# Attention score products of a head pair, alternating between the lower and the upper 64 rows of the array

## The chip, the cores and the metric

The kernel runs on one core of a Trainium2 chip. The metric is the device time of one execution in microseconds. Before the change the median of three runs is 2363.9 us (2360.26 to 2368.31). The five engines of the core work from queues of their own and meet through semaphores: TensorE (PE; its weight loads are listed apart as PEld), VectorE (DVE), ScalarE (ACT), GpSimd (POOL) and SyncE (SP), which here only starts DMAs.

## The reference, cut to what matters

One layer, 512 prompt tokens and 32 sample tokens, width 1024. The part that the change touches is the attention over the prompt: three groups of eight heads of 64 channels, each group with a window and a dilation of its own, and one softmax over the keys of all three groups of a head slot.

```python
HEAD_DIM = 64
HEADS_PER_GROUP = 8
GROUP_WINDOWS = (128, 512, 2048)
GROUP_DILATIONS = (1, 4, 16)
...
    s = jnp.einsum('brnqhe,brnkhe->brnhqk', qb, kb, preferred_element_type=F32) * (HEAD_DIM ** -0.5)
    s = jnp.where(mask[None, None, :, None], s, -jnp.inf)
    lse = jax.nn.logsumexp(s, axis=-1)
    p = jnp.exp(s - lse[..., None]).astype(v.dtype)
    o = jnp.einsum('brnqhk,brnkhe->brnqhe', p, vb).reshape(b, dilation, mp, h, e)[:, :, :m]
...
def finish_layer(x, heads_out, conv_out, gates, w_attn_proj, w_out, norm2_w,
                 w_peer_q, peer_sub_keys, expert_u, expert_v):
    attn_out = heads_out.reshape(b, t, ATTN_OUT_WIDTH) @ w_attn_proj
    mixed = gates[:, :, 0] * conv_out + gates[:, :, 1] * attn_out
    x1 = x + mixed @ w_out
    h2 = rms_norm(x1, norm2_w)
    return x1 + peer(h2.reshape(b * t, D_MODEL), w_peer_q, peer_sub_keys,
                     expert_u, expert_v).reshape(b, t, D_MODEL)
```

The last step, `peer`, gathers 128 experts per token from a table of 16384 rows. All arithmetic is float32.

## The kernel before

The 512 prompt tokens are four tiles of 128 (t = 0 to 3); the 32 sample tokens are a fifth, `NT`. Work runs in two phases: phase 0 takes tiles 0, 1 and `NT` through the whole layer up to the expert search, phase 1 takes tiles 2 and 3. The gathers of the experts (544 steps of 128 rows of 8 KB) of tiles 0, 1 and `NT` run beside phase 1, those of tiles 2 and 3 mostly after it.

`plan()` (L204) writes out the order of all work by hand as a list of ticks. A tick holds one `mm` entry (usually two of the eight slices of a projection) and whatever other tasks were put on it. Each engine walks through all the ticks in order and does its own part of each task; inside a tick the tasks stand by the rank in `RANK` (L199): the projection first, the score task `S` after `T` (turn the weights), `O` (weights times values), `H` and `M`. `pe_cost` and `step_marks` (L395, L403) spread the gather steps over the ticks: `MARK[n]` is the number of gather steps that PE has to have done by tick n.

Attention goes by head slot x = 8t + 2hp + w: hp is one of four pairs, w one of two heads of a pair. The queries and keys of a pair lie in the same tiles, head 0 on partitions 0 to 63 and head 1 on 64 to 127, so a score product contracts over 64 rows. `rounds(t)` (L101) cuts the key blocks of a slot into rounds of at most four blocks (512 columns, one PSUM bank): two rounds for tiles 0 to 2, three for tile 3. For each round `scores` (L1151) on PE waits until its bank is free, multiplies the runs of neighbouring blocks into it and raises `s_ready`; DVE scales, masks and copies the bank to `s_sb` (L1931). There are two score banks, `sbk`, used in turn by every user of the pool (`SB`, made by `bank_uses`, L496): `S`, and also `DS` (sample attention), `L1`, `L2`, `W` and `SC`. After the last round DVE takes the maximum (`M`, L1941), ACT the exponential (L1586), PE turns the weights (L1343) and multiplies the values (L1173).

In `plan()` the loop over w (L279) puts the rounds of head 0 on consecutive ticks from `at`, its `M` on the next, and then the rounds of head 1. For the first pair of tile 0 this is: rounds of head 0 at ticks 65 and 66, `M` at 67, rounds of head 1 at 68 and 69, `M` at 70; tile 1 follows with 71, 72, 73 and 74, 75, 76. The four pairs of phase 0 start 27 ticks apart, those of phase 1 24 ticks apart (from tick 322 on). `first` (L297), the tick from which the sample attention of phase 0 (`DS`, `DN`, `DM`, `DT`, `DV`, `DE`, `DH`) and the norm of the sample tokens are put, is the tick after the last `M`: 158.

```python
                    for w in range(2):
                        x = HG * t + 2 * hp + w
                        for r in range(len(rounds(t))):
                            put(at + r, ("S", x, r))
                        at += len(rounds(t))
                        put(at, ("M", x))
```

The q and k projections go through two banks `zb`. The reader that frees such a bank is `q2` on DVE (L1907), put three ticks after the end of the projection; POOL computes its scale in `q1` (L1038, L1039) from a sum that DVE makes (L1896).

Of the kernel before, what the change touches and what calls it, by code (L numbers as in the profile page):

```python
# [13 lines left out]
P = 128  # L14
# [8 lines left out]
HD, HG, NG = 64, 8, 3  # L23
# [77 lines left out]
def rounds(t):  # L101


    g1 = [(1, u) for u in range(t + 1)]
    g2 = [(2, t)] + [(2, u) for u in range(t)]
    g0 = [(0, u) for u in (t - 1, t) if u >= 0]
    if t == 3:
        return [(0, g1), (6, g2), (4, g0)]
    return [(3 - t, g1 + g0[:-1]), (5, g0[-1:] + g2)]
# [18 lines left out]
def turn_groups(t):  # L128
    return -(-len(blocks_of(t)) // 4)
# [6 lines left out]
def pair(x):  # L136

    t, r = divmod(x, HG)
    return t, r // 2, r % 2
# [64 lines left out]
def plan():  # L204
# [5 lines left out]
    def put(tick, task):  # L210
        tasks.setdefault(int(tick), []).append(task)
# [26 lines left out]
    for p in range(2):  # L238
# [21 lines left out]
        free_at = 0  # L260
        for hp in range(HP):
            for ty in range(3):
                for t, e in each(p, "qkv", hp, ty):
                    if ty < 2:
                        put(e + 1, ("q1", t, hp, ty))
                        put(e + 3, ("q2", t, hp, ty))
                        put(e + 4, ("q3", t, hp, ty))
                        put(e + 6, ("Q", t, hp, ty))
                        if ty == 1:
                            put(e + 6, ("ko", t, hp))  # L270
                        continue
                    put(e + 1, ("v", t, hp))
                    put(e + 2, ("vo", t, hp))
                    if p == 0 and t != NT:
                        put(e + 4, ("hs", t, hp))
                    if t == NT:
                        continue
                    at = max(e + 4, free_at)
                    for w in range(2):  # L279
                        x = HG * t + 2 * hp + w  # L280
                        for r in range(len(rounds(t))):
                            put(at + r, ("S", x, r))
                        at += len(rounds(t))
                        put(at, ("M", x))
                        for q in range(turn_groups(t)):
                            put(at + 2 + q, ("T", x, q))
                        put(at + 3 + turn_groups(t), ("O", x))
                        put(at + 4 + turn_groups(t), ("E", x))
                        last = at + 6 + turn_groups(t)
                        at += 1  # L290
                    free_at = at
                    put(last, ("H", x))
            if p and hp < 2:
                put(last + 1, ("hl", hp + 2))
            if p == 0 and hp == 2:
                put(now, ("kv", 0))
        first = free_at  # L297
        for q in range(4):
            for t, e in each(p, "gate", q):
                put(e + 1, ("g", t, q))  # L300
# [224 lines left out]
ZB, SB, TB, OB = bank_uses()  # L525
# [68 lines left out]
def program(nc, a, sc):  # L594
    with ExitStack() as ctx:
# [45 lines left out]
        qT = qTs[:, :].rearrange("p (a b g t) -> p a b g t", a=2, b=2, g=NG)  # L641
        kT = kvr[:, 0:8 * QW].rearrange("p (a g t) -> p a g t", a=2, g=NG)
# [72 lines left out]
        sbk = [ps("s0"), ps("s1")]  # L715
# [10 lines left out]
        s_ready, s_free = sem("s_ready"), [sem("s_free_v"), sem("s_free_a")]  # L726
# [40 lines left out]
        def bank_free(eng, pool, by_sems, key):  # L767
            at = pool.before(key)
            if at is not None:
                eng.wait_ge(by_sems[at[0]], at[1])  # L770
# [333 lines left out]
        def _(eng):  # L1104
# [44 lines left out]
                    mm.then_inc(z_ready, 1)  # L1149

            def scores(x, r):  # L1151
                t, hp, w = pair(x)
                lo = HD * w
                if r == 0:
                    eng.wait_ge(tp_free, TB.no["Q", t, hp, 1] + 1)
                    if t % 2:
                        eng.wait_ge(tp_free, TB.no["Q", t - 1, hp, 1] + 1)
                    if t >= 2 and w == 0:
                        eng.wait_ge(hist_in[hp % 2], 32 * (hp // 2 + 1))
                bank_free(eng, SB, s_free, ("S", x, r))  # L1160
                bank = sbk[SB.bank(("S", x, r))]
                for at, g, u, c in runs(rounds(t)[r][1]):
                    mm = eng.matmul(bank[:, P * at:P * (at + c)], qT[lo:lo + HD, hp % 2, t % 2, g, :], kT[lo:lo + HD, hp % 2, g, P * u:P * (u + c)], start=True, stop=True)  # L1163
                mm.then_inc(s_ready, 1)

            def weigh(x):
                t, hp, w = pair(x)
# [130 lines left out]
            for n, tick in enumerate(TICKS):  # L1298
                for v in tick:
                    if v[0] == "mm":  # L1300
                        multiply(*v[1:])
                    elif v[0] == "XT":
                        t, q = v[1:]
# [4 lines left out]
                        for j in range(4):  # L1308
                            mm = eng.transpose(tpb[:, P * j:P * j + m], rows[:, 512 * q + P * j:512 * q + P * (j + 1)], cst[0:m, C_ID:C_ID + m])
                        mm.then_inc(tp_ready, 1)  # L1310
                    elif v[0] == "U":
                        t, c = v[1:]
# [3 lines left out]
                        if t == NT:  # L1316
                            for r in range(QUAD):
                                lo = 64 * (r % 2)
                                mm = eng.matmul(tpb[lo:lo + 64, P * (r // 2):P * (r // 2) + SMP], ub[:, i % 2, 0:64], ident[:, SMP * r:SMP * (r + 1)], start=True, stop=True)
# [13 lines left out]
                                mm = eng.transpose(tpb[:, P * g:P * (g + 1)], qkr[:, t % 2, ty, P * g:P * (g + 1)], ident)  # L1333
                        mm.then_inc(tp_ready, 1)
                    elif v[0] == "S":
                        scores(*v[1:])
                    elif v[0] == "T":
                        x, q = v[1:]
                        nb = len(blocks_of(pair(x)[0]))
# [768 lines left out]
```

## Time and profile before

| what | value |
| --- | --- |
| median of 3 runs | 2363.9 us |
| the profiled execution's own time | 2364.97 us |
| its span, first to last instruction | 2363.1 us |
| PE busy | 1678.2 us (71%) |
| DVE busy | 1468.1 us (62%) |
| mean granted TensorE clock | 0.801 |

The profiled execution lies 1.1 us above the median and 1.9 us above its own span. A view by stretches tells at what share of its time each engine was busy and which clock PE had; the list of waits tells who waited for whom; the timeline gives starts and durations in order; the chain follows the work that ended last back to what released it. The end of a matmul is modelled and includes its drain, so what a group of matmuls costs in the stream is read from its start to the start of the next group.

### The profile page before, as it was taken

To read this page: it belongs to the slowest core of one execution; us is meant where nothing else is said; L and a number is where in the kernel's file an instruction comes from. 1 tells how busy PE (TensorE), PEld (TensorE's weight loads), DVE (VectorE), ACT (ScalarE), POOL (GpSimd) and SP (SyncE) were. 2 spreads that over 40 slices of the span, in tenths; PEclk is the share of its full clock that TensorE was granted. 3 is DMA by queue.
4 is the path that set the end of the run, shared out by engine and by line. 5 is a ranking of instruction groups with operands and counts; after the bars stand their busy time and mean duration, and the time that the engine had idled before them with its cause. 6 is when DMAs were issued, how large, how long until landed. Compare 5 with 4: busy or idle time off the path is not lost.

```text
span 2363.1 us, 32781 instructions
## 1 busy us (share of the span) xinstructions
PE 1678.2 (71%) x11544; PEld 770.1 (33%) x11544; DVE 1468.1 (62%) x3591; ACT 882.9 (37%) x2386; POOL 750.7 (32%) x713
## 2 busy tenths in 40 slices
PE   6988899998788887777788889885433343343343
PEld 3455565444334443433444433331000000000000
DVE  1466656212556777777878676535676765676764
ACT  2122123201444544544455662333343333343332
POOL 1244100000222334433343333323444443344342
PEclk9998999999889998898889999996555555555555
DMA  4333435645889888899989999999999999999998
GB/s 170 137 105 105 158 111 216 263 182 191 310 345 383 345 350 326 314 347 358 339 343 359 367 394 397 404 407 371 408 391 405 401 392 376 400 387 399 403 386 362
DMA packets 130191, 756.64 MB, mean 320 GB/s; under 512 B 16836, under 2 KB 42940, under 8 KB 50268
## 3 DMA queue, kind: packets, MB, share of 16 engines
q0 software_dynamic: 78336, 570.46, 61.5%
q1 hardware_dynamic: 51692, 184.09, 21.0%
q8 instruction: 92, 1.51, 0.2%
q14 instruction: 71, 0.58, 0.1%
HBM read 734.70 MB, written 20.64 MB: 320 GB/s over the span
## 4 chain that ended last, share of the span: by engine, by line
DMA 20%; DVE 15%; PE 9%; issue 6%; ACT 3%; POOL 0%; DVEq 0%; POOLq 0%; ACTq 0%
DMA ring<-in_expert_uv,pick 20%; PE z L1141 4%; DVE ring L1843 4%; PE acc L1292 3%; DVE cand L1785 1%; DVE e L1786 1%; DVE cand L1783 1%; DVE ti L1748 1%; DVE ti L1751 1%; DVE sco L1749 1%; ACT wgt L1455 1%; ACT fold L1457 1%; DVE tv L1750 1%; DVE ci L1751 1%; DVE ci L1748 1%
## 5 line engine op out<-in xcount | busy, mean ns | idle before, releaser
L1073 POOL DMA_INDIRECT ring<-in_expert_uv,pick x544 | 628.1, 1155 | 1012.2 <-PE acc L1292 935.1
L1843 DVE CUSTOM_DVE_ANT_0 ring<-ring,rep 128x1024 f32<-128x1024 f32 x544 | 660.3, 1225 | 379.1 <-DMA ring<-in_expert_uv,pick 354.5
L1292 PE MATMUL acc<-ring,fold 128*32 128x256 f32 x4352 | 464.0, 517 | 496.9 <-ACT fold L1457 495.0
L1141 PE MATMUL z<-wts,hT 128*128 128x384 f32 (+1 forms) x1408 | 628.4, 583 | 31.7 <-DVE tmp L1907 25.3
L1453 ACT ACTIVATE gel<-dots 128x1 f32<-128x1 f32 x544 | 109.8, 202 | 790.7 <-DVE dots L1843 783.2
L1292 PEld LDWEIGHTS acc<-ring,fold 128*32 128x32 f32 x4352 | 105.3, 126 | 822.1 <-ACT fold L1457 746.8
L1141 PEld LDWEIGHTS z<-wts,hT 128*128 128x128 f32 x1408 | 263.8, 203 | 288.6 <-issue 229.4
L1141 PE MATMUL z<-wts,yT 128*128 128x512 f32 x384 | 192.2, 636 | 14.3 <-ACT yT L1631 7.0
L1457 ACT ACTIVATE fold<-cst,wgt 128x32 f32<-128x32 f32 x544 | 174.8, 321 | 17.7
L1455 ACT ACTIVATE wgt<-gel,pick 128x1 f32<-128x1 f32 x544 | 160.3, 295 | 17.7
L1740 DVE SCALAR_TENSOR_TENSOR yT<-uT,vec,yT 128x256 f32<-128x256 f32 x240 | 109.2, 504 | 2.0
L1141 PEld LDWEIGHTS z<-wts,yT 128*128 128x128 f32 x384 | 70.8, 199 | 102.0 <-issue 101.9
L1931 DVE SCALAR_TENSOR_TENSOR sx<-s,cst 128x512 f32<-128x512 f32 (+3 forms) x72 | 40.2, 558 | 97.8 <-PE s L1163 91.0
L1038 POOL TENSOR_SCALAR xss<-xss 128x1 f32<-128x1 f32 (+1 forms) x10 | 1.9, 194 | 302.1 <-ACT kvr L1646 247.9
L1453 ACT ACT_TABLE_LOAD x69 | 88.5, 1283 | 1.2
L1038 POOL TENSOR_SCALAR ssq<-ssq 128x6 f32<-128x6 f32 (+1 forms) x40 | 15.4, 386 | 196.7 <-DVE ssq L1896 196.1
L1163 PE MATMUL s<-kvr,qTs 64*128 64x128 f32 (+3 forms) x272 | 68.0, 369 | 0.0
L1466 ACT ACTIVATE pt<-t 128x512 f32<-128x512 f32 (+2 forms) x64 | 33.4, 522 | 79.0 <-PE t L1343 79.0
L1173 PEld LDWEIGHTS o<-kvr,pt 128*128 128x128 f32 x432 | 55.2, 200 | 17.9 <-issue 11.0
L1173 PE MATMUL o<-kvr,pt 128*128 128x64 f32 x432 | 54.4, 279 | 8.1 <-DVEq L1810 5.8
L1343 PE MATMUL t<-cst,sx 128*128 128x128 f32 x216 | 39.5, 303 | 21.3 <-ACT hoT L1466 17.1
L1039 POOL TENSOR_TENSOR ssq<-ssq,half_m 128x6 f32<-128x6 f32 (+1 forms) x40 | 49.8, 1246 | 3.5 <-POOL ssq L1038 0.2
(219 smaller groups left out, 1745.2 us busy)
## 6 DMA issues: line engine op xcount, KB each, us to landing
wts<-in_w_qkv SPq DMA_DIRECT2D x24, 1536.0 KB, 8.2
wts<-in_w_glu SPq DMA_DIRECT2D x8, 2048.0 KB, 12.2
wts<-in_w_gate SPq DMA_DIRECT2D x8, 2048.0 KB, 11.6
wts<-in_w_wq SPq DMA_DIRECT2D x8, 2048.0 KB, 11.7
ring<-in_k_cache SPq DMA_DIRECT2D x8, 1536.0 KB, 9.4
ring<-in_v_cache SPq DMA_DIRECT2D x8, 1536.0 KB, 8.1
rep<-x_h SPq DMA_DIRECT2D x68, 128.0 KB, 9.9
ring<-in_expert_uv,pick POOLq DMA_INDIRECT x544, 11.3
```

The source lines that it names most:

```text
L1039: return eng.tensor_tensor(to, to, half_m[0:m, 0:w], ALU.pow)
L1073: eng.indirect_dma_start(ring[:, i % RING, :], None, a["expert_uv"], bass.IndirectOffsetOnAxis(picks(i, 0).bitcast(U32), 0)).then_inc(row_ ...
L1141: mm = eng.matmul(bank[:, 0:w], of[:, k, :], rows[:, k, :], start=(k == 0), stop=(k == depth - 1))
L1163: mm = eng.matmul(bank[:, P * at:P * (at + c)], qT[lo:lo + HD, hp % 2, t % 2, g, :], kT[lo:lo + HD, hp % 2, g, P * u:P * (u + c)], start=T ...
L1173: mm = eng.matmul(ob[:, 0:HD], pt[:, P * j:P * (j + 1)], vv[:, hp % 2, u, P * g + HD * w:P * g + HD * (w + 1)], start=(j == 0), stop=(j == ...
L1292: mm = eng.matmul(acc[b][SUB * c:SUB * (c + 1), col:col + 256], fold[:, i % 4, :], ring[:, i % RING, D + 256 * c:D + 256 * (c + 1)], start ...
L1453: eng.activation(gel[:, i % 4:i % 4 + 1], dots[:, i % 4:i % 4 + 1], ACT.Gelu).then_inc(gel_ready, 1)
L1455: eng.activation(wgt[:, i % 4:i % 4 + 1], gel[:, i % 4:i % 4 + 1], ACT.Copy, scale=picks(i, 1)).then_inc(wgt_ready, 1)
L1457: eng.activation(fold[:, i % 4, :], cst[:, C_FOLD:C_FOLD + SUB], ACT.Copy, scale=wgt[:, i % 4:i % 4 + 1]).then_inc(fold_ready, 1)
L1740: ins = eng.scalar_tensor_tensor(out=out, in0=src, scalar=cw[:, c, tap:tap + 1], in1=out, op0=ALU.mult, op1=ALU.add)
L1748: link(eng.max_index(index[:, 0:8], values[:, 0:8], x))
L1843: eng.tensor_tensor_reduce(u, u, rep[:, j, :], 1.0, 0.0, ALU.mult, ALU.add, dots[:, i % 4:i % 4 + 1]).then_inc(dot_ready, 1)
```

## The change

In the planner the rounds of both heads of a pair are put on the same ticks, first head then second, and the `M` and later tasks of the second head follow the first head's by one tick and as many ticks as the first head has turns (`turn_groups`: 1 for tile 0, 2 for tiles 1 and 2, 3 for tile 3). `free_at` keeps the next tile behind the turns of the second head. `first` becomes the tick after the last score round. On PE the `S` entry of the second head does nothing; the entry of the first head waits for both banks and issues the products of both heads in turn, run by run: head 0 from rows 0 to 63 into its bank, head 1 from rows 64 to 127 into the other. One increment by 2 on the last product tells DVE of both. DVE's copies are unchanged but for their ticks.

```diff
--- before.py
+++ after.py
@@ -276,25 +276,28 @@
                     if t == NT:
                         continue
                     at = max(e + 4, free_at)
+                    for r in range(len(rounds(t))):
+                        for w in range(2):
+                            put(at + r, ("S", HG * t + 2 * hp + w, r))
+                            scored = at + r + 1
                     for w in range(2):
                         x = HG * t + 2 * hp + w
-                        for r in range(len(rounds(t))):
-                            put(at + r, ("S", x, r))
-                        at += len(rounds(t))
+                        if w == 0:
+                            at += len(rounds(t))
                         put(at, ("M", x))
                         for q in range(turn_groups(t)):
                             put(at + 2 + q, ("T", x, q))
                         put(at + 3 + turn_groups(t), ("O", x))
                         put(at + 4 + turn_groups(t), ("E", x))
                         last = at + 6 + turn_groups(t)
-                        at += 1
-                    free_at = at
+                        at += 1 + (1 - w) * turn_groups(t)
+                    free_at = at + turn_groups(t)
                     put(last, ("H", x))
             if p and hp < 2:
                 put(last + 1, ("hl", hp + 2))
             if p == 0 and hp == 2:
                 put(now, ("kv", 0))
-        first = free_at
+        first = scored
         for q in range(4):
             for t, e in each(p, "gate", q):
                 put(e + 1, ("g", t, q))
@@ -1149,19 +1152,22 @@
                     mm.then_inc(z_ready, 1)
 
             def scores(x, r):
-                t, hp, w = pair(x)
-                lo = HD * w
+                t, hp, _ = pair(x)
                 if r == 0:
                     eng.wait_ge(tp_free, TB.no["Q", t, hp, 1] + 1)
                     if t % 2:
                         eng.wait_ge(tp_free, TB.no["Q", t - 1, hp, 1] + 1)
-                    if t >= 2 and w == 0:
+                    if t >= 2:
                         eng.wait_ge(hist_in[hp % 2], 32 * (hp // 2 + 1))
-                bank_free(eng, SB, s_free, ("S", x, r))
-                bank = sbk[SB.bank(("S", x, r))]
+                banks = []
+                for w in range(2):
+                    bank_free(eng, SB, s_free, ("S", x + w, r))
+                    banks.append(sbk[SB.bank(("S", x + w, r))])
                 for at, g, u, c in runs(rounds(t)[r][1]):
-                    mm = eng.matmul(bank[:, P * at:P * (at + c)], qT[lo:lo + HD, hp % 2, t % 2, g, :], kT[lo:lo + HD, hp % 2, g, P * u:P * (u + c)], start=True, stop=True)
-                mm.then_inc(s_ready, 1)
+                    for w in range(2):
+                        lo = HD * w
+                        mm = eng.matmul(banks[w][:, P * at:P * (at + c)], qT[lo:lo + HD, hp % 2, t % 2, g, :], kT[lo:lo + HD, hp % 2, g, P * u:P * (u + c)], start=True, stop=True)
+                mm.then_inc(s_ready, 2)
 
             def weigh(x):
                 t, hp, w = pair(x)
@@ -1333,7 +1339,8 @@
                                 mm = eng.transpose(tpb[:, P * g:P * (g + 1)], qkr[:, t % 2, ty, P * g:P * (g + 1)], ident)
                         mm.then_inc(tp_ready, 1)
                     elif v[0] == "S":
-                        scores(*v[1:])
+                        if pair(v[1])[2] == 0:
+                            scores(*v[1:])
                     elif v[0] == "T":
                         x, q = v[1:]
                         nb = len(blocks_of(pair(x)[0]))
```

## Rows read from the trace of the kernel before

**Rows 1.** The stretches: us, busy time (instructions) by engine, PEclk, DMA share, GB/s.

```profile
138.00:355.00 217.00, 198.57 (x1243) 129.60 (x1242) 130.37 (x309) 50.80 (x117) 50.85 (x71) 0.93 0.36 122
355.00:575.00 220.00, 211.59 (x1485) 106.20 (x1487) 65.07 (x138) 44.28 (x80) 2.23 (x6) 1.00 0.58 216
...
880.00:1320.00 440.00, 346.77 (x1960) 176.17 (x1956) 342.06 (x863) 221.87 (x534) 169.45 (x142) 0.87 0.90 340
...
1625.00:2363.00 738.00, 294.74 (x2296) 62.43 (x2296) 488.37 (x1184) 264.94 (x868) 303.64 (x264) 0.52 0.99 390
```

**Rows 2.** Waits of PE, then of DVE, from 138 to 355 us: total, times, longest.

```profile
PE z L1141 <- DVE tmp L1907: 16.5, 6, 3.5
...
DVE sx L1931 <- PE s L1163: 52.9, 29, 6.0
```

**Rows 3.** Waits of PE, then of DVE, from 880 to 1320 us.

```profile
PE acc L1292 <- ACT fold L1457: 28.4, 14, 4.4
...
DVE sx L1931 <- PE s L1163: 38.1, 20, 7.0
```

**Rows 4.** The score products (L1163) alone in two stretches: PE busy, PEld busy.

```profile
138.00:355.00 217.00, 24.34 (x128) 17.76 (x128) 0.93 0.36 122
880.00:1320.00 440.00, 43.61 (x144) 21.34 (x144) 0.87 0.90 340
```

**Rows 5.** Timeline of PE, phase 0: start, us, line, tile, shape, count.

```profile
155.54 0.93 PE L1163 MATMUL s<-kvr,qTs 64*128 64x128 f32 x6
156.41 0.91 PE L1141 MATMUL z<-wts,hT 128*128 128x384 f32 x2
```

**Rows 6.** Timeline of PE, phase 1: a score product and four products on 32 columns.

```profile
1201.02 0.70 PE L1163 MATMUL s<-kvr,qTs 64*128 64x256 f32 x2
1201.65 0.64 PE L1292 MATMUL acc<-ring,fold 128*32 128x256 f32 x8
1202.22 0.59 PE L1141 MATMUL z<-wts,hT 128*128 128x384 f32 x1
```

**Rows 7.** Timeline, DVE and PE, around PE's wait in phase 0.

```profile
161.93 0.56 DVE L1931 SCALAR_TENSOR_TENSOR sx<-s,cst 128x384 f32<-128x384 f32 x1
...
164.08 0.56 DVE L1931 SCALAR_TENSOR_TENSOR sx<-s,cst 128x384 f32<-128x384 f32 x1 [0.22 <-PE s L1163]
...
166.84 0.55 DVE L1907 TENSOR_TENSOR tmp<-z,ssq 128x384 f32<-128x384 f32 x1
...
167.53 0.98 PE L1141 MATMUL z<-wts,hT 128*128 128x384 f32 x1 [3.49 <-DVE tmp L1907]
```

**Rows 8.** Chain that ended last, second heads' score products, from 1116 us: start, us.

```profile
1151.92 1.06 PE s L1163 x4
1155.48 1.09 PE s L1163 x6
...
1197.11 1.08 PE s L1163 x4
...
1309.86 1.06 PE s L1163 x4
1314.28 0.64 PE s L1163 x2
```

**Rows 9.** Timeline, PE and DVE: two rounds of a head and the copy between.

```profile
1161.46 1.12 PE L1163 MATMUL s<-kvr,qTs 64*128 64x512 f32 x2
...
1169.34 1.13 PE L1163 MATMUL s<-kvr,qTs 64*128 64x128 f32 x4
...
1169.71 0.69 DVE L1931 SCALAR_TENSOR_TENSOR sx<-s,cst 128x512 f32<-128x512 f32 x1
```

**Rows 10.** Who waited for DVE's copies (L1931) in the whole run.

```profile
  PEld s L1163: 0.2, 1
```

**Rows 11.** Waits of PE from 355 to 575 us.

```profile
PE s L1190 <- DMA ring<-in_k_cache: 2.0, 1, 2.0
```

**Rows 12.** DMA issues of the page: loads, KB each, median us from issue to landing.

```profile
wts<-in_w_gate SPq DMA_DIRECT2D x8, 2048.0 KB, 11.6
```

## Prediction

> **What bounds the kernel now.** I read the stretches first: they say where PE sets the pace. From 138 to 355 us lie the projections of phase 0 with its attention. PE is busy for 198.6 of 217 us there, DVE for 130 and the DMA engines for 0.36 of the time; from 355 to 575 us PE is busy for 211.6 of 220 us [rows 1]. So phase 0 goes at PE's pace, and what PE saves there moves everything behind it, unless a wait of PE takes it. The list of waits has one that matters: PE waits 16.5 us in six places for DVE to free a projection bank [rows 2]. From 880 to 1320 us, the attention of phase 1, no engine is full: PE 347 of 440 us, DVE 342, DMA share 0.90 [rows 1]. PE waits there for weights that come of the gathers (28.4 us), and DVE in turn waits 38.1 us in 20 places for score products [rows 3]. From 1625 us on the DMA share is 0.99 [rows 1]: a fixed number of gathers, which the change doesn't touch. A gain can only come out of the two attention stretches, and it shifts the tail as a whole.
>
> **The score products.** By the view of L1163 alone they take 24.3 us of PE in phase 0 and 43.6 us in phase 1 [rows 4]. These times hold drains: a round of 0.93 us is followed by the next group after 0.87 [rows 5], one of 0.70 after 0.63 [rows 6], so 0.07 us of each round isn't stream time. There are 32 rounds in phase 0 (four pairs, two tiles, two heads, two rounds) and 40 in phase 1 (tile 3 has three): 24.3 - 2.2 = 22.1 us and 43.6 - 2.8 = 40.8 us.
>
> The change leaves as many products, but sends them in pairs to separate halves of the array's rows. No row of this trace has two products on different rows at once, so the cost is bounded from both sides. Nothing gained: the two halves run one after the other, and the saving is 0. Everything gained: a pair of rounds costs what one does, and half is saved, 11.0 and 20.4 us. A cost above today's is the fourth case below. The nearest row is one on columns: eight instructions of 256 columns on four strips of 32 columns start and give way to the next group within 0.57 us (1201.65 to 1202.22), while two instructions of 256 columns on 64 rows and all columns took 0.63 us (1201.02 to 1201.65) [rows 6]. So four float32 products in four parts of the array cost what one does, and they are issued in turn, part by part, as the change does it with rows. I take the upper end, half. The Trainium skill (TensorE: Matmul & The Clock Gate, Part 3: Packing small matmuls — row/col tiling) gives 3.07 times for four row tiles, less than the full four; as an estimate from that page two tiles would give 1.54 times, a saving of 35% instead of half, and the forecast's gain of 17 us would be about 12. No run so far shows row tiles.
>
> **Phase 0: what of 11.0 us reaches the end.** PE sets the pace, so all of it, except where PE waits afterwards for something that hasn't become earlier. That is the wait of 3.49 us at 167.53 us [rows 7], right behind the score rounds of tile 1's second head; it occurs in three of the four pairs (the fourth has gates behind it, whose bank DVE doesn't free). PE waits for DVE's q2 (166.84 us). Before that DVE does two score copies of 0.56 us, one at 161.93 and one at 164.08 us, the second after waiting for PE [rows 7]. In the new order both copies come three ticks earlier, where DVE is ahead of PE anyway (it waits for PE in 29 of the 32 rounds of phase 0, 52.9 us [rows 2]), so q2 comes 1.1 us earlier. PE comes to the wait about 1.7 us earlier (two rounds of 0.87 [rows 5]). The wait keeps 0.6 us of each, 1.8 us in three. Left: 11.0 - 1.8 = 9.2 us.
>
> **Phase 1: what of 20.4 us reaches the end.** The chain that ended last can be followed back to 1116 us, so it covers pairs 2 and 3. Of the second heads' ten rounds there, which are what pairing folds away, five stand on the chain: 1.06 + 1.09 + 1.08 + 1.06 + 0.64 = 4.9 us [rows 8]. The others stand beside DVE's or ACT's work, which is late next, and bring nothing. For all four pairs I take twice that, 9.9 us; the ends are 0 (the gathers and DVE set the pace, DMA share 0.90) and 20.4.
>
> **The new wait.** Today a round waits for the copy made two rounds earlier; DVE's copies have held up PE for 0.2 us in the whole run [rows 10]. In the new order a pair takes both banks, and the next round, one tick later, needs both copies done. Behind the waiting product PE holds the next projection slices, the gather products and the turns; for those wait ACT, DVE and, for its ring buffers, POOL. Phase 0: two copies of 0.56 us [rows 7] are 1.1 us; the tick between holds four projection instructions, of which two take 0.91 us with their drain [rows 5], so they cover it and the cost is 0. Without that cover it would be 1.1 us in each of eight places, 9 us, the whole gain of phase 0. Phase 1 has twelve such places. The longest lag of DVE: the round that starts at 1161.46 and streams for 1.06 us is copied only from 1169.71 on, 7.2 us later; with two copies of 0.69 us the banks would be free after 8.6 us, and PE comes to the next round after 6.8 us (1169.34) [rows 9]. That is 1.8 us here; elsewhere the lag is shorter and the tick covers it. I take 2 us; bounds 0 and the fourth case.
>
> **Small parts.** The sample attention and the norm of the sample tokens of phase 0 start at tick 154 instead of 158 with their distances kept; the cache loads that SP starts behind them, and SP's waits for them, move along. One of these loads now comes ahead of the weights of the last gate unit (ticks 165 and 166), which PE needs nine ticks later; a gate load lands 11.6 us after its issue [rows 12], and nine ticks of four instructions at some 0.4 us [rows 5] are over 14 us without the sample products between them. PE's one wait there for a key cache is 2.0 us [rows 11], so -2 to +2, taken as 0. In phase 1 tile 3's attention lies two ticks later; its turns, values and the history load for pair hp+2 that SP starts after it have more than ten ticks to spare before their users. Gather steps shift by a few ticks with the score cost; their number and their sum stay. The increment by 2 lets DVE start on the first head only when both are done; with the halves side by side that is nothing. Where PE gains time but then waits, its granted clock, 0.87 in this stretch [rows 1], may fall; 0.01 of it is at most 347 x 0.01 / 0.87 = 4 us of PE's busy time there, in either direction; taken as 0.
>
> **The sum.** 9.2 + 9.9 - 2 = 17.1 us. From the profiled execution's own 2364.97 us: 2347.9. That execution lies 1.1 us above the median of 2363.9, so against the median the forecast is -16 us, 0.7%. About 0.3% (7 us) is what a measurement of this kernel can tell from no change.
>
> **The rivals.** First: the halves overlap, but phase 1 gives nothing. For it speak the DMA share of 0.90, PE's 28.4 us of waiting for weights from the gathers and the fact that DVE is as busy as PE [rows 1, 3]; against it that five second-head rounds stand on the chain [rows 8]. 2365 - 9 = 2356 us.
>
> Second: the change doesn't do what it says, row halves don't overlap. PE's stream stays at 22.1 and 40.8 us. For it: no row shows it. Against: the column strips [rows 6]. 2365 us, give or take 4 for the moved copies and the two banks.
>
> Third: phase 1 passes on all: 2365 - 9 - 20 + 2 = 2338 us.
>
> Fourth, slower: two banks used at once take the place of the double buffer, and PE waits for DVE. If DVE were as far behind in all twelve places of phase 1 as at 1161.46 us, the banks would be free after 8.6 us. PE comes back after 6.8 us in the eight places of tile 3 [rows 9] and in the four of tile 2 after a tick of four projection instructions and one gather group, 4 x 0.45 + 0.57, about 2.3 us [rows 5, 6]: 8 x 1.8 + 4 x 6.3 = 40 us, less 17: 2388 us. It decides from 1.4 us per place on (17 / 12). Against it: DVE waited for PE, not PE for DVE, in 20 of these 40 rounds [rows 3]. The Trainium skill (TensorEngine Tiling (Array Packing), PSUM Bottleneck) warns of just that: a faster array leaves the copy out of PSUM as the bottleneck. By that rule it would be this case; by DVE's 52.9 us of waiting for PE in phase 0 [rows 2] the copies there have room.
>
> **Chances.** Forecast 0.55, phase 1 nothing 0.17, no overlap 0.15, all passed on 0.05, slower 0.08. A time more than 7 us below the median means under 2357: nearly all of the forecast, half or more of the first rival and the third: 0.53 + 0.11 + 0.05 = 0.69. Within 7 us: 0.02 + 0.06 + 0.11 = 0.19. Slower: 0.04 + 0.08 = 0.12. The range from 2335 to 2366 takes in the forecast, the first and third rivals and half of the second.
>
> **What the profile would show.** Right: pairs of score instructions of the two halves start within a few hundredths of a microsecond, L1163's busy time falls from 68 us to about 36, the sample attention starts 8 to 10 us earlier, and the stretch from 575 to 1625 us shrinks by about as much again. The new wait would stand as PE or PEld s L1163 <- DVE sx, under 5 us. Wrong: L1163's time stays (second rival), the tail starts no more than 9 us earlier (first), or PE's waits for DVE's copies reach 17 us (fourth).

## The result and the profile after

The changed kernel takes 2342.09 us in the median of five runs (2335.23 to 2347.16) against 2363.9 before (now five runs too, 2360.26 to 2374.4). The ratio of the two is 0.9894, with a 95% interval from 0.9868 to 0.992: faster by about 1%, 22 us in the medians and 25 by the ratio. The forecast was 16 us, to 2348. The profiled execution took 2339.12 us, with a span of 2337.3 us and a mean granted clock of 0.797.

The lines move by a few: the scores are L1169, their copies L1938, the projections L1144, the expert products L1298, `q2` L1914, the dot products of the gathered rows L1850. First the stretches of the changed kernel, cut where the work of [rows 1] is done (columns as there):

```profile
138.00:350.00 212.00, 191.37 (x1284) 122.33 (x1283) 134.10 (x322) 49.65 (x114) 51.60 (x70) 0.93 0.37 127
350.00:565.00 215.00, 207.59 (x1438) 104.68 (x1440) 60.11 (x126) 45.47 (x81) 2.22 (x6) 1.00 0.58 218
...
865.00:1300.00 435.00, 340.26 (x2039) 171.42 (x2037) 352.59 (x894) 231.11 (x557) 165.49 (x149) 0.88 0.93 359
...
1600.00:2337.00 737.00, 292.08 (x2288) 61.56 (x2288) 486.61 (x1182) 264.70 (x867) 304.76 (x264) 0.52 0.99 390
```

The tail is as long as before and as full (DMA share 0.99, as in [rows 1]); it only starts earlier. Phase 0 is still PE's. In the attention of phase 1 the DMA share has risen from 0.90 to 0.93.

The score products alone in the two attention stretches, PE and PEld busy, against 24.34 and 43.61 us in [rows 4]:

```profile
138.00:350.00 212.00, 12.28 (x128) 9.04 (x128) 0.93 0.37 127
865.00:1300.00 435.00, 22.25 (x144) 10.68 (x144) 0.88 0.93 359
```

Half, in both. PE's timeline shows it on single rounds, one of phase 0 and one of phase 1:

```profile
153.45 0.94 PE L1169 MATMUL s<-kvr,qTs 64*128 64x128 f32 x12
154.32 1.56 PE L1144 MATMUL z<-wts,hT 128*128 128x384 f32 x4
...
943.16 0.70 PE L1169 MATMUL s<-kvr,qTs 64*128 64x256 f32 x4
943.79 0.64 PE L1298 MATMUL acc<-ring,fold 128*32 128x256 f32 x8
```

Twelve instructions of both heads (two for each product) take 0.87 us from their start to the next group's, as six of one head did in [rows 5]; four take 0.63 us, as two did in [rows 6]. In the records of the single instructions the partner on the other rows starts in most pairs 6 to 8 ns after its neighbour.

PE's wait for a projection bank, which [rows 7] show at 3.49 us, on the timeline of the changed kernel (DVE's `q2`, then PE):

```profile
163.16 0.56 DVE L1914 TENSOR_TENSOR tmp<-z,ssq 128x384 f32<-128x384 f32 x1
...
163.86 1.91 PE L1144 MATMUL z<-wts,hT 128*128 128x384 f32 x4 [3.56 <-DVE tmp L1914]
```

and its total in the list of PE's waits from 138 to 350 us (total, times, longest):

```profile
PE z L1144 <- DVE tmp L1914: 17.6, 6, 4.0
```

The three waits of that kind are now 3.56, 3.96 and 3.81 us; before, each was 3.49. The total has grown from 16.5 to 17.6 us [rows 2].

What `q2` itself waits for has changed. The end of POOL's scale and DVE's maximum of the second head in the kernel before, where `q2` starts at 166.84 us [rows 7]:

```profile
163.78 1.33 POOL L1039 TENSOR_TENSOR ssq<-ssq,half_m 128x6 f32<-128x6 f32 x1
...
165.26 0.95 DVE L1941 TENSOR_REDUCE nm<-sx 128x1 f32<-128x768 f32 x1
```

and in the changed one, where it starts at 163.16:

```profile
161.50 1.44 POOL L1042 TENSOR_TENSOR ssq<-ssq,half_m 128x6 f32<-128x6 f32 x1
...
161.98 0.95 DVE L1948 TENSOR_REDUCE nm<-sx 128x1 f32<-128x768 f32 x1
```

Before, `q2` came 1.7 us after the scale was done (165.11; spans on POOL are rough), behind the maximum; now it comes 0.2 us after it (162.94), and the maximum runs beside POOL's work.

Who waited for DVE's score copies, in the whole run (total, times), against 0.2 us once in [rows 10]:

```profile
  PEld s L1169: 4.8, 7
  PE s L1169: 1.1, 1
```

The first line is that of PE's weight loads (PEld), the second that of its products, and the two are not to be added up. The weight load and the product of the round at 1125.79 us wait for the same copies:

```profile
1125.76 0.78 PEld L1169 LDWEIGHTS s<-kvr,qTs 64*128 64x128 f32 x12 [1.14 <-DVE sx L1938]
1125.79 1.15 PE L1169 MATMUL s<-kvr,qTs 64*128 64x128 f32 x12 [1.08 <-DVE sx L1938]
```

The other six weight loads are like the first one in phase 0, whose products (153.45 us, above) waited for nothing:

```profile
153.45 0.75 PEld L1169 LDWEIGHTS s<-kvr,qTs 64*128 64x128 f32 x12 [0.55 <-DVE sx L1938]
```

In all six the products start 0.42 or 0.52 us after the last projection instruction, as score rounds behind such instructions did before. So DVE's copies hold up PE's products for 1.1 us in one place of phase 1, and nowhere else.

How long DVE waits for score products, first in phase 0 (138 to 350 us), then in phase 1 (865 to 1300 us); before, it was 52.9 and 38.1 us [rows 2, 3]:

```profile
DVE sx L1938 <- PE s L1169: 39.9, 16, 7.7
...
DVE sx L1938 <- PE s L1169: 11.4, 5, 5.1
```

Where the time was gained is best read from the dot products of the gathered rows, since their first one needs the expert search of phase 0 done and their last one stands at the end of the tail. This is their line in the kernel before (shortest, median and longest in ns, then first and last start in us):

```profile
L1843 DVE CUSTOM_DVE_ANT_0 ring<-ring,rep x544: 1211/1225/1296, 595.2 to 2355.6; 128x1024 f32<-128x1024 f32 x182
```

and in the changed one:

```profile
L1850 DVE CUSTOM_DVE_ANT_0 ring<-ring,rep x544: 1210/1225/1297, 585.6 to 2329.8; 128x1024 f32<-128x1024 f32 x182
```

Phase 0 gave 9.6 us (595.2 to 585.6). From the first dot to the last the run is another 16.2 us shorter; since the medians differ by 22 us and the two profiled executions by 26, phase 1 gave some 12 to 16 us.

### The profile page after: what moved, and what is told of

It reads as the page before. It is cut to its first block, busy times and chain, and to the rows that moved or that the text cites. A ratio compares the mean times of both kernels' runs of the same rounds, so it can differ in the third digit from the quotient of the medians.

```text
span 2337.3 us, 32787 instructions
## 1 busy us (share of the span) xinstructions
PE 1648.7 (71%) x11544; PEld 752.6 (32%) x11544; DVE 1465.3 (63%) x3591; ACT 883.0 (38%) x2386; POOL 745.9 (32%) x713
## 4 chain that ended last, share of the span: by engine, by line
PE 35%; DMA 27%; DVE 24%; issue 8%; ACT 4%; POOL 2%; SPq 0%; DVEq 0%; POOLq 0%; ACTq 0%
DMA ring<-in_expert_uv,pick 24%; PE z L1144 21%; DVE ring L1850 6%; PE acc L1298 4%; DMA sx<-in_x_prompt 2%; PE z L1150 2%; PE o L1179 1%; PE o L1232 1%; DVE cand L1792 1%; DVE e L1793 1%; DVE ti L1755 1%; PE s L1196 1%; DVE ti L1758 1%; DVE sco L1756 1%; DVE cand L1790 1%
## 5 line engine op out<-in xcount | busy, mean ns | idle before, releaser
L1076 POOL DMA_INDIRECT ring<-in_expert_uv,pick x544 | 614.9, 1130 | 998.6 <-PE acc L1298 920.5
L1850 DVE CUSTOM_DVE_ANT_0 ring<-ring,rep 128x1024 f32<-128x1024 f32 x544 | 660.3, 1225 | 387.9 <-DMA ring<-in_expert_uv,pick 357.4
L1298 PE MATMUL acc<-ring,fold 128*32 128x256 f32 x4352 | 460.6, 514 | 503.5 <-ACT fold L1464 501.8
L1144 PE MATMUL z<-wts,hT 128*128 128x384 f32 (+1 forms) x1408 | 627.6, 584 | 38.1 <-DVE tmp L1914 31.9
L1298 PEld LDWEIGHTS acc<-ring,fold 128*32 128x32 f32 x4352 | 105.0, 125 | 825.7 <-ACT fold L1464 756.2
L1144 PEld LDWEIGHTS z<-wts,hT 128*128 128x128 f32 x1408 | 265.8, 203 | 296.4 <-issue 238.4
L1144 PE MATMUL z<-wts,yT 128*128 128x512 f32 x384 | 191.2, 633 | 13.2 <-ACT yT L1473 6.4
L1144 PEld LDWEIGHTS z<-wts,yT 128*128 128x128 f32 x384 | 70.2, 198 | 100.0 <-issue 99.9
L1041 POOL TENSOR_SCALAR ssq<-ssq 128x6 f32<-128x6 f32 (+1 forms) x40 | 20.5, 513 | 193.3 <-DVE ssq L1903 192.7
L1938 DVE SCALAR_TENSOR_TENSOR sx<-s,cst 128x512 f32<-128x512 f32 (+3 forms) x72 | 36.8, 552 | 53.3 <-PE s L1169 51.3
L1042 POOL TENSOR_TENSOR ssq<-ssq,half_m 128x6 f32<-128x6 f32 (+1 forms) x40 | 52.9, 1322 | 3.5 <-POOL ssq L1041 0.2
L1593 ACT ACTIVATE sx<-sx,nm 128x384 f32<-128x384 f32 (+3 forms) x32 | 32.5, 1015 | 52.6 <-DVE nm L1949 52.5
## 6 DMA issues: line engine op xcount, KB each, us to landing
ring<-in_expert_uv,pick POOLq DMA_INDIRECT x544, 11.3
```

The source lines that it names most:

```text
L1042: return eng.tensor_tensor(to, to, half_m[0:m, 0:w], ALU.pow)
L1076: eng.indirect_dma_start(ring[:, i % RING, :], None, a["expert_uv"], bass.IndirectOffsetOnAxis(picks(i, 0).bitcast(U32), 0)).then_inc(row_ ...
L1144: mm = eng.matmul(bank[:, 0:w], of[:, k, :], rows[:, k, :], start=(k == 0), stop=(k == depth - 1))
L1298: mm = eng.matmul(acc[b][SUB * c:SUB * (c + 1), col:col + 256], fold[:, i % 4, :], ring[:, i % RING, D + 256 * c:D + 256 * (c + 1)], start ...
L1850: eng.tensor_tensor_reduce(u, u, rep[:, j, :], 1.0, 0.0, ALU.mult, ALU.add, dots[:, i % 4:i % 4 + 1]).then_inc(dot_ready, 1)
```

## Experiments

Every kernel was compared with runs of the kernel before on its own chip, where the median of before was 2371.5, 2367.7 or 2366.3 us; so the ratios are what can be set side by side. "Changed" is the kernel with the change.

**Both heads on the same rows.** The planner's new order, the pairs and the two banks stay; only the overlap is taken away, in both phases.

```diff
-                        lo = HD * w
+                        lo = 0
```

> The changed kernel, but the products of both heads are taken from rows 0 to 63 (so the second head's scores are those of the first); order, banks, waits and ticks are those of the changed kernel. Theory (the gain is the overlap of the row halves): the score products cost PE some 63 us of stream again, twice the changed kernel's, and the time is that of the kernel before, 2364 us, within 5. Rival (the gain comes of the new order of the ticks: DVE's copies earlier, fewer places where DVE waits for PE): most of the 22 us stay, 2342 to 2350 us.

Measured: 2352.58 us, ratio 0.9924 [0.9898, 0.995], 18 us by the ratio, of the 25 or 26 of the change. The stream of the scores in the two stretches:

```profile
138.00:352.00 214.00, 20.15 (x128) 16.62 (x128) 0.93 0.34 117
865.00:1330.00 465.00, 40.69 (x144) 23.12 (x144) 0.88 0.92 356
```

and the round on PE's timeline that answers to the twelve instructions above:

```profile
153.79 1.60 PE L1169 MATMUL s<-kvr,qTs 64*128 64x128 f32 x12
155.33 1.24 PE L1144 MATMUL z<-wts,hT 128*128 128x384 f32 x3
```

On the same rows the twelve instructions take 1.54 us instead of 0.87, so the overlap is real, and it is the rows that bring it. But the order alone is already faster than before, and has more than half of the gain. Two things were seen at once. In phase 0, of the 12.1 us of busy time that the scores lost (24.34 to 12.28), 4.2 came of pairing without any overlap (24.34 to 20.15). About 1.1 of these are the drains of 16 groups fewer, 0.07 us each as the prediction counts them, and 3 are stream: two rounds apart cost twice 0.87 us, a pair on the same rows 1.54, so what lies between groups is paid once instead of twice. And the other part of this kernel's gain has little to do with the stream: the scores of phase 1 are still busy for 40.69 us here (36.8 and 36.5 in the two runs below with the same phase 1; three rounds took 4.2 us longer here).

**The same rows in phase 1 only.** The overlap of phase 0 stays. It ran twice, on two chips.

```diff
-                        lo = HD * w
+                        lo = HD * w if t < 2 else 0
```

> The changed kernel with both heads' products from rows 0 to 63 in phase 1 alone (tiles 2 and 3), so that the halves overlap in phase 0 only; the second head's scores of tiles 2 and 3 are the first's. Theory (9 to 10 us of the gain are phase 0's, the rest is stream time saved in phase 1): 2354 us. Rival (phase 1's gain is not the stream time but the new order): 2342 to 2346 us.

> The kernel with both heads of tiles 2 and 3 taken from rows 0 to 63 once more, now beside the changed kernel on one chip. Theory A (the first runs' reading: phase 1's gain comes of the new order, in which DVE waits for PE in fewer places and a pair pays the first weight load and the switch behind it once, not of the overlap): within 4 us of the changed kernel. Theory B (the forecast's: half of the stream saved reaches the end): the stream in phase 1 is 12 us longer than in the changed kernel, so 6 us slower than that; if all of it reaches the end, 12 us.

> The changed kernel itself, measured beside the next three on one chip. All theories: about 1% below the kernel before on the same chip.

Measured: 2346.03 us, 0.9888 [0.9859, 0.9918], and beside the changed kernel itself 2342.51 us, 0.99 [0.9883, 0.9916], where the changed kernel had 2340.04 us, 0.9889 [0.9867, 0.991]. The score products of phase 1 in the second run of this kernel:

```profile
865.00:1330.00 465.00, 36.48 (x144) 21.11 (x144) 0.89 0.93 357
```

and in the changed kernel beside it:

```profile
865.00:1330.00 465.00, 21.58 (x144) 10.69 (x144) 0.87 0.93 357
```

PE streams 14.9 us more, and the end comes 2.5 us later in the medians; the single executions of the two kernels put the difference between -3 and 7 us, so it isn't told from 0, and half of the stream, 7.4 us, lies at the edge. The first run of this kernel, at 0.9888, isn't slower than the change either. So in phase 1 the overlap itself brings little, and nothing that can be measured here. Against the kernel with the same rows in both phases, on its chip, the first run is 6.6 us faster (2352.58 to 2346.03) for the 7.9 us of stream that differ in phase 0. The dot products of these two kernels, same rows in both phases first:

```profile
L1850 DVE CUSTOM_DVE_ANT_0 ring<-ring,rep x544: 1212/1225/1294, 590.7 to 2343.3; 128x1024 f32<-128x1024 f32 x182
...
L1850 DVE CUSTOM_DVE_ANT_0 ring<-ring,rep x544: 1211/1225/1294, 584.3 to 2339.3; 128x1024 f32<-128x1024 f32 x182
```

Their first one comes 6.4 us earlier with the overlap in phase 0: there most of the saving does reach the end. With the old phase 0 it starts on the same chip at 595.7 us (the next experiment), so without any overlap the new order already gives 5 us of phase 0.

**The change in one phase only.** A function of the tile decides between the changed order with its pairs and the old one, here for phase 0, with the opposite condition for phase 1.

```diff
+def paired(t):
+    return t < 2
...
+                    if paired(t):
+                        for r in range(len(rounds(t))):
+                            for w in range(2):
+                                put(at + r, ("S", HG * t + 2 * hp + w, r))
...
+                    else:
+                        for w in range(2):
+                            x = HG * t + 2 * hp + w
+                            for r in range(len(rounds(t))):
+                                put(at + r, ("S", x, r))
```

> Pairs in phase 0 alone; tiles 2 and 3 keep the plan and the products of the kernel before. Theory: 9 to 10 us less than before, 2354 us, and the tail of gathers starts some 10 us earlier than before. Rival (the halves' gain of phase 0 is swallowed by the gathers behind it): 2360 us or more.

> Pairs in phase 1 alone; tiles 0 and 1 keep the plan and the products of the kernel before. By the forecast's own step (half of 20 us reaches the end, less 2 us of waits) 2356 us. By the profile after (phase 1 gave 16 us) 2348 us. If the profiled run was an outlier of the kernel, in between: 2352 us.

Measured: phase 0 only, 2362.68 us, 0.9964 [0.9944, 0.9984], 8.5 us by the ratio; phase 1 only, 2353.68 us, 0.9934 [0.9909, 0.9958], 15.6 us. Together they make the whole (0.9964 x 0.9934 = 0.9898; the change measured 0.9894 and 0.9889). The dot products with phase 0 only, the first 9.7 us earlier than before, the last only 1.4:

```profile
L1888 DVE CUSTOM_DVE_ANT_0 ring<-ring,rep x544: 1211/1225/1298, 585.5 to 2354.2; 128x1024 f32<-128x1024 f32 x182
```

and with phase 1 only, the first where it was, the last 8.9 us earlier:

```profile
L1888 DVE CUSTOM_DVE_ANT_0 ring<-ring,rep x544: 1210/1225/1297, 595.7 to 2346.7; 128x1024 f32<-128x1024 f32 x182
```

The first starts fit phase 0: with the old one they are 593.1 to 595.7 us in three profiled executions, with the changed one 579.8 to 585.6 in seven, of which the two under 584 had a granted clock of 0.95 and 0.96 from 130 to 356 us, all the others 0.93. The last ones stand for one execution each, and scatter as the executions do (2351.9 to 2370.5 us for the first of the two kernels), so the sizes are taken from the ratios.

**The old order, tile 3's attention two ticks later.** The kernel before, with nothing paired and no overlap; only the distance that the change puts ahead of tile 3 is kept.

```diff
-                    at = max(e + 4, free_at)
+                    at = max(e + 4, free_at + 2 * (t == 3))
```

> The kernel before with tile 3's attention put two ticks later, as the change does by the way, and nothing else of the change. Theory (DVE's fewer waits are what phase 1 gains by): no difference from the kernel before, within 4 us. Rival (the spacing is what gains): 8 us or more below it.

Measured: 2359.32 us, 0.9963 [0.9946, 0.9979], 8.8 us by the ratio. An edit of one line to the kernel before, which removes no work, is worth as much as all of phase 0. DVE's waits for scores don't explain it: in phase 1 they are 43.7 us in 18 places here and 38.1 in 20 before [rows 3]. What differs is another wait, at the products that spread an index list into the output bank that DVE's normalised heads (`ho`) free. On the timeline of the kernel before, the longest of them:

```profile
1017.80 0.28 DVE L1951 TENSOR_SCALAR ho<-o,rden 128x64 f32<-128x64 f32 x1
...
1018.14 0.29 PE L1274 MATMUL o<-cand,cst 32*32 32x8 f32 x8 [7.36 <-DVE ho L1951]
```

its line in that kernel's list of PE's waits from 865 to 1330 us:

```profile
PE o L1274 <- DVE ho L1951: 13.5, 3, 7.4
```

and the same line with tile 3 two ticks later:

```profile
PE o L1274 <- DVE ho L1951: 1.3, 2, 0.8
```

It goes through all the kernels: the one with the change in phase 0 only, whose phase 1 is the old one, has 13.3 us of it in three places; in the changed kernel and those with the same rows, the change in phase 1 only or other small shifts it is 2.6 us at most. So the spacing moves the spread out of the way of a head that isn't normalised yet. That this one wait is the whole 8.8 us is not shown: PE's wait for the experts' weights fell too (28.4 to 15.1 us), and no run took the one away without the other. Nor does any run take the two ticks out of the changed kernel; that they are worth as much there is assumed.

**Another two ticks, in the changed kernel.** The same edit once more, on top of the change.

> The changed kernel with tile 3's attention another two ticks later. If spacing as such pays (the old order gained 0.37% by it), another 4 to 8 us below the changed kernel. If only the first two ticks pay, because they take tile 3's first copies away from tile 2's turns, no difference (within 3 us).

Measured: 2344.51 us, 0.9895 [0.9872, 0.9918]: no further gain, as follows if the wait at the spread was already gone. It showed something else. Who waited for DVE's copies:

```profile
  PEld s L1169: 11.3, 8
  PE s L1169: 7.1, 3
```

PE's products wait 7.1 us in three places, against 1.1 in one; eight weight loads show 11.3 us, three of them in the same three places. That is less than the 17 us at which the prediction would have given up its forecast, but six times the wait of the changed kernel, and the time is that of the changed kernel. So either such waits cost nothing that can be measured, or the added ticks gained what the waits cost; no run separates the two. DVE waits 23.7 us for scores here, twice as long as in the changed kernel.

**Pairs of rounds two ticks apart in phase 1.** A tick of projection and gather work more between two pairs, so that DVE has done both copies.

```diff
-                            put(at + r, ("S", HG * t + 2 * hp + w, r))
-                            scored = at + r + 1
+                            put(at + gap(t) * r, ("S", HG * t + 2 * hp + w, r))
+                            scored = at + gap(t) * r + 1
...
-                            at += len(rounds(t))
+                            at += gap(t) * (len(rounds(t)) - 1) + 1
```

with `gap(t)` 1 for tiles 0 and 1 and 2 for the others.

> The changed kernel with the rounds of a pair two ticks apart instead of one in phase 1, so that DVE has two ticks to free both banks. The profile after shows PE's products waiting for DVE's copies 5.9 us in 8 places; these should go. Forecast's fourth case in small: at most 4 us below the changed kernel, more likely within 3 of it, as the maxima come later by one or two ticks.

Measured: 2353.46 us, 0.9944 [0.992, 0.9968], over half a percent slower than the changed kernel (0.9889). Who waited for the copies:

```profile
  PEld s L1174: 2.4, 4
```

and in the list of waits of phase 1, DVE's for scores and PE's for the experts' weights:

```profile
DVE sx L1943 <- PE s L1174: 26.6, 8, 6.8
...
PE acc L1303 <- ACT fold L1469: 45.0, 24, 6.4
```

No product waits for the copies any more (1.1 us in the changed kernel; the 2.4 us are the four weight loads of phase 0, whose products don't wait), and the stream is as short as in the changed kernel (21.03 us), yet time is lost. The edit also ends the scores and puts the maxima one tick later for tile 2 and three for tile 3, whose attention starts a tick later besides (the expectation has one or two ticks, and takes the new wait at 5.9 us), and more waiting stands at the experts' weights (45.0 us, 31.5 in the changed kernel over the same stretch); that the one leads to the other is likely and not shown. At any rate the change's new wait is cheaper than this way to avoid it.

**Head by head.** The two loops inside a round are exchanged: all products of the first head, then all of the second, on their own rows and banks, without alternation.

```diff
-                for at, g, u, c in runs(rounds(t)[r][1]):
-                    for w in range(2):
+                for w in range(2):
+                    for at, g, u, c in runs(rounds(t)[r][1]):
```

> The changed kernel with the loops over runs and heads exchanged: all products of the first head of a round, then all of the second, on their own rows; nothing else differs. If PE overlaps only neighbours in its order, rounds with one run keep the overlap, those with two or three overlap at one place only: L1163's stream would be about 14 of 22 us in phase 0 and 28 of 41 in phase 1 instead of 11 and 23, and the time 3 to 5 us above the changed kernel. If PE looks further ahead, no difference.

Measured: 2343.16 us, 0.9901 [0.9884, 0.9918]; the changed kernel beside it had 0.9889. The stream in both stretches:

```profile
130.00:352.00 222.00, 13.63 (x128) 10.45 (x128) 0.94 0.38 130
865.00:1330.00 465.00, 22.88 (x144) 11.85 (x144) 0.88 0.93 359
```

and on PE's timeline a round of two runs a head, then one of three:

```profile
148.81 0.93 PE L1169 MATMUL s<-kvr,qTs 64*128 64x256 f32 x8
149.67 1.56 PE L1144 MATMUL z<-wts,hT 128*128 128x384 f32 x4
151.16 1.26 PE L1169 MATMUL s<-kvr,qTs 64*128 64x128 f32 x12
152.35 1.56 PE L1144 MATMUL z<-wts,hT 128*128 128x384 f32 x4
```

The round of two runs overlaps as well as with alternation (0.86 us here, 0.85 in the changed kernel); the one of three runs takes 1.19 us, against 0.87 alternating and 1.54 on the same rows. In all, alternation is worth 1.4 us of stream in phase 0 and about 1 in phase 1 (the changed kernel's two profiles have 22.25 and 21.58 us there), and 3 us of the end in the medians, inside the intervals. PE finds the overlap mostly by itself.

**The second head's maximum of tile 1 two ticks later.** This was to move DVE's maximum out of the way of `q2`, which ends PE's wait in phase 0. The head's turns and values move with it.

```diff
+                        at += 2 * (t == 1 and w == 1)
                         put(at, ("M", x))
```

> The changed kernel with the maximum of tile 1's second head two ticks later in phase 0, behind DVE's q2 for which PE waits 3.6 to 4.0 us in three pairs. Theory (q2 stands in DVE's queue behind that maximum, 1.1 us): the three waits fall to about 2.7 us each, 3 us less in all. Rival (q2 waits for POOL's scale, not for its place in the queue): the waits stay, no difference.

Measured: 2334.38 us, 0.9863 [0.9838, 0.9888]. PE's wait for `q2` in phase 0:

```profile
PE z L1145 <- DVE tmp L1915: 16.3, 6, 3.7
```

The three waits are 3.74, 3.67 and 3.51 us: 0.4 us less in all, so the maximum is not what holds `q2`. That fits the timeline above, where `q2` follows POOL's scale by 0.2 us. The time is the lowest median of all, but its interval overlaps the changed kernel's.

**The sample attention where it was.** In the changed kernel `first` is put back from tick 154 to 158.

```diff
-        first = scored
+        first = scored + 4
```

> The changed kernel with the sample attention of phase 0 back at its old tick 158. By the forecast (taken as 0, bounds -2 to +2): no difference, within 3 us of the changed kernel.

Measured: 2336.27 us, 0.9861 [0.9837, 0.9886]. Its interval too overlaps the changed kernel's: the four ticks cost nothing and bring nothing that can be measured. Neither this kernel nor the one above is shown to beat the change.

## Why the prediction was right, and where its steps were not

**The stream, right.** Row halves overlap fully: 24.34 to 12.28 us and 43.61 to 22.25, where the prediction took half as the upper end, by the column strips of [rows 6]. The second rival falls with it. The estimate from the Trainium skill (TensorE: Matmul & The Clock Gate, Part 3), a saving of 35%, was too low for two halves of the rows: half against two separate rounds, and 43% against both heads in one group on the same rows (1.54 to 0.87 us). The measurement decides. What the prediction didn't see is that a part of phase 0's saving, 4.2 of 12.1 us of busy time, comes from having 16 groups fewer, and would have come on the same rows.

**Phase 0, right in size.** 9.2 us were forecast; the first dot product came 9.6 us earlier, and the change in phase 0 alone gave 8.5 by the ratio. The wait for `q2` behaved as said but kept less: the three grew by 0.86 us in all (11.33 from 10.47), not 1.8. With the copies earlier, `q2` comes nearly as much earlier as PE does, until POOL's scale holds it. The overlap has no part in it: with the same rows the three waits are 3.55, 3.93 and 3.80 us.

**Phase 1, right in sign, wrong in mechanism.** The step that failed is that about half of the stream that is saved reaches the end, because five of ten second-head rounds stand on the chain [rows 8]: 9.9 less 2, 7.9 us. Measured were 12 to 16. With the overlap taken away in phase 1 alone, the medians differ by 2.5 us, not told from 0; so the term for the stream should have been small, as the first rival said, whose reasons (DMA share 0.90, PE waiting for weights of the gathers, [rows 1, 3]) were the better ones. The first rival's time, 2356, was wrong all the same, because it thought of the stream only. The gain came from the order, which the prediction had under the small parts, as "tile 3's attention lies two ticks later", at 0. Those two ticks alone are 8.8 us [5 to 13] in the old order, and they go with the end of a wait of 13.5 us at the index spreads. That wait was to be seen in the trace before, in the list of which [rows 3] show the first line; the prediction took up the waits that the scores touch and left that one out, though the planner's lines move its cause.

The rest of phase 1, the ratio of the change (0.9889) against the product of phase 0 alone and the spacing alone (0.9964 x 0.9963 = 0.9927), is about 9 us, give or take 8 by the three intervals, if the parts add up. Some 2 of it may be the overlap. The rest would go with the two heads' scores coming together, in the same order on the same ticks, which no run tries alone. A reason suggests itself, that DVE gets its scores in time (its wait fell from 38.1 to 11.4 us, and the kernel at two ticks, with 26.6, is slower); but with another two ticks ahead of tile 3 it waits 23.7 us and nothing is lost. Which of DVE's waits carries it stays open.

**The new wait, small as said.** 2 us were taken for phase 1 and 0 for phase 0; PE's products wait 1.1 us in one place of phase 1, and none in phase 0. The lines themselves, 4.8 and 1.1 us, are under the 5 that the prediction named. The fourth rival's mechanism exists, therefore, but at that one place only, far from the 17 us from which it was to decide. In the kernel with another two ticks it is 7.1 us, and the time doesn't differ measurably. The Trainium skill's warning (TensorEngine Tiling (Array Packing), PSUM Bottleneck) that the copy may become the bottleneck behind a faster array shows here as this wait of 1.1 us, and no further.

**The small parts.** The sample attention starts 17.6 us earlier (339.0 us, from 356.6), not 8 to 10: the prediction's own list of signs left out the four ticks that it had named. With the four ticks taken back, the time does not rise. The cost at 0 was right. PE's wait for a key cache is still 2.0 us [rows 11], and the granted clock of phase 1 is 0.88, after 0.87 before [rows 1].

**The sum.** 9.2 for 9.6, and 7.9 for 12 to 16: 17 us forecast, 22 in the medians and 26 between the two profiled executions. The time lies within the range, and the sign rests on the part of the reasoning that held, phase 0. That the sum came so near is luck: a term for phase 1's stream of which next to nothing was measured stood in for a gain of the order that had been put at 0.

## What to carry to other kernels

Two float32 products of 64 rows each cost what one costs here, on different row halves and into different banks; that was worth most of its size where TensorE sets the pace (some 6.5 of 7.9 us in phase 0), and nothing that could be measured beside the gathers (2.5 of 14.9 us in phase 1, inside the intervals). Where an order is written out by hand, an edit of it is two edits: before crediting the faster instruction, try the new places alone, in the old kernel, and the new order with the old instruction. And read every line of the list of waits in the stretch whose ticks move, also those that the changed operation has no part in.

## What was not expected of the hardware

PE overlaps the row halves without being handed the products in turn: head by head, rounds of two runs a head take 0.86 us, as alternating, and only rounds of three runs lose, 1.19 us against 0.87. The records of the single instructions (two for each product) show how. In rounds of two runs the second head's first instruction starts 13 to 15 ns after the first head's first, with three of the first head's still waiting ahead of it. In rounds of three runs it starts only 6 or 7 ns after the first head's third, again with three ahead. So PE starts a product of the other half although products of the first half stand before it and haven't started, but in none of these 24 rounds past more than three instructions. And a group of products of its own costs about 0.2 us beside its stream (two rounds of 0.87 us against 1.54 us for both in one group on the same rows).
